# The compression's first weights as units of the weight ring, in a fused two-layer kernel on one core

## What is computed

```python
u = rms_norm(h, norm_mix_pre[l])
(q_n, kc_n, vc_n, ks_n, vs_n, kw_n, vw_n, g_n,
 q_s, k_s, v_s, gate_a, gate_b) = jnp.split(u @ w_in[l], IN_OFFSETS, axis=-1)
kc = compress_kv(kvr(kc_n), cmp_pos_k[l], cmp_w1_k[l], cmp_w2_k[l])
vc = compress_kv(kvr(vc_n), cmp_pos_v[l], cmp_w1_v[l], cmp_w2_v[l])
o_a = nsa_attention(q_n..., kc, vc, ks_n, vs_n, kw_n, vw_n, g_n, bias_nsa)
o_b = swa_sink_attention(q_s, k_s, v_s, attn_sinks, bias_swa)
y = sigmoid(gate_a) * (o_a @ w_up_nsa) + sigmoid(gate_b) * (o_b @ w_up_swa)
h = h + rms_norm(y @ w_out, norm_mix_post)
...
def compress_kv(kv, pos, w1, w2):   # 15 overlapping blocks of 32 tokens, 2 groups
    ...
    return jax.nn.gelu(flat @ w1) @ w2      # flat 30 x 2048, w1 2048 x 256
```

## Time and profile before

| | us |
|---|---|
| Median of 3 runs | 1580.57 (1578.18 to 1581.78) |
| The profiled execution | 1580.16 |
| Its span in the trace | 1578.4 |
| Mean granted TensorE clock | 0.987 of 2.4 GHz |
| PE busy | 1525.8 |
| DVE busy | 1028.0 |
| ACT busy | 835.6 |
| POOL busy | 349.9 |
| Read from HBM | 250.23 MB |

### The profile page before, as it was taken

The page is one execution under the profiler, slowest core; times in us unless marked ns, Lnnn a source line. Parts: engine busy times, 40 slices in busy tenths (PEclk is TensorE's granted clock), DMA queues, the critical chain, the costliest instruction groups (busy, mean ns, idle before and its releaser), DMA issues.

```text
span 1578.4 us, 29131 instructions
## 1 busy us (share of the span) xinstructions
PE 1525.8 (97%) x11414; PEld 1428.1 (90%) x11414; DVE 1028.0 (65%) x1792; ACT 835.6 (53%) x1638; POOL 349.9 (22%) x403
## 2 busy tenths in 40 slices
PE   7799999999989989999999999999999999999998
PEld 6389999999988989999999999999999888888886
DVE  4255567555677864577999967777774555555554
ACT  4166455444456543445444457777775555554544
POOL 1132421000255553411455540011112000000000
PEclk9899999999998999999999999999999999999999
DMA  9732354555443532355445554444445555555553
GB/s 213 229 108 95 135 191 162 183 179 186 147 129 101 164 123 81 101 178 192 147 162 175 172 181 153 138 144 137 145 135 171 189 198 189 197 191 197 190 197 135
DMA packets 76773, 254.23 MB, mean 161 GB/s; under 512 B 11375, under 2 KB 15293, under 8 KB 76509
## 3 DMA queue, kind: packets, MB, share of 16 engines
q1 hardware_dynamic: 76397, 251.71, 48.5%
q0 software_dynamic: 240, 0.66, 0.2%
HBM read 250.23 MB, written 1.84 MB: 160 GB/s over the span
## 4 chain that ended last, share of the span: by engine, by line
PE 79%; DVE 12%; DMA 2%; ACT 2%; POOL 2%; issue 1%; SPq 0%; POOLq 0%; DVEq 0%; ACTq 0%
PE bank L675 78%; DVE wl L1667 4%; DVE big L1667 3%; POOL big L2347 1%; DMA big<-in_w1k 1%; ACT big L1242 1%; DVE big L1670 1%; ACT wh L1242 1%; DVE big L2193 1%; DVE big L2204 1%; DVE big L2200 1%; DVE big L2189 1%; DVE big L2210 1%; DVE big L2197 1%; PE bank L990 1%
## 5 line engine op out<-in xcount | busy, mean ns | idle before, releaser
L1667 DVE TENSOR_TENSOR wl<-raw,wh 128x1024 fp32r<-128x1024 f32 (+4 forms) x459 | 532.1, 1160 | 397.5 <-ACT wh L1242 397.0
L1242 ACT ACTIVATE wh<-raw 128x1024 fp32r<-128x1024 f32 (+1 forms) x459 | 482.2, 1053 | 347.9 <-PE bank L675 330.3
L675 PE MATMUL bank<-gw,wh 128*128 128x256 f32 x3504 | 652.8, 288 | 2.7 <-DVE big L1670 2.7
L675 PEld LDWEIGHTS bank<-gw,wh 128*128 128x128 f32 x3504 | 548.7, 193 | 3.5 <-DVE big L1670 3.1
L675 PE MATMUL bank<-gw,wl 128*128 128x256 f32 x1752 | 498.5, 285 | 6.1 <-POOL wl L2347 5.0
L675 PEld LDWEIGHTS bank<-gw,wl 128*128 128x128 f32 x1752 | 337.7, 193 | 7.8 <-issue 6.3
L675 PE MATMUL bank<-xw,wh 128*128 128x256 f32 x1696 | 322.9, 291 | 9.7 <-ACT wh L1242 7.9
L675 PE MATMUL bank<-wh,xw 128*128 128x512 f32 x1056 | 326.9, 391 | 0.0
L675 PEld LDWEIGHTS bank<-xw,wh 128*128 128x128 f32 x1696 | 268.7, 195 | 17.3 <-ACT wh L1242 8.2
L1242 ACT ACTIVATE big<-bank 128x256 f32<-128x256 f32 (+23 forms) x326 | 118.2, 372 | 259.9 <-PE bank L675 221.7
L2347 POOL TENSOR_TENSOR wl<-raw,wh 128x384 fp32r<-128x384 f32 (+3 forms) x131 | 175.4, 1345 | 333.2 <-ACT wh L1242 333.1
(11 more groups left out here) (136 smaller groups left out, 1096.4 us busy)
## 6 DMA issues: line engine op xcount, KB each, us to landing
raw<-in_wst SPq DMA_DIRECT2D x455, 512.0 KB, 3.5
big<-toeplitz SPq DMA_DIRECT2D x8, 256.0 KB, 14.0
big<-in_w1k SPq DMA_DIRECT2D x4, 512.0 KB, 18.3
big<-in_w1v SPq DMA_DIRECT2D x4, 512.0 KB, 19.1
big<-in_xT SPq DMA_DIRECT2D x4, 256.0 KB, 5.4
raw<-in_wst SPq DMA_DIRECT2D x4, 256.0 KB, 5.1
big<-in_keys SPq DMA_DIRECT2D x1, 1024.0 KB, 5.4
out<-big SPq DMA_DIRECT2D x4, 256.0 KB, 2.4
```

What stands on the lines that cost most here:

```text
L675: return e.matmul(o, a, b, start=first, stop=last, skip_group_check=True)
L1242: return e.activation(o, x, f, **kw)
L1667: return e.tensor_tensor(o, a, b, f)
```

## The change

1. The eight pieces of w1 become units 14, 16, ..., 28 of the ring (`W1_AT`); UNITS goes from 457 to 465. Each shares a slot with an ordinary unit before it (13, 15, 17, 19: queries of the second attention; 21 to 27: four of the `GA` gates). They are split into halves as all units are, and TensorE's new `compress` makes 8 products for each behind the slot's last quarter: the inputs' high and low halves side by side (60 columns) by `WH`, and the high half (30 columns) by `WL`. The inputs' halves are `CXW`, in the free second half of `GW`: two copies on ScalarE and two subtractions on VectorE. `H60` takes the sums; four products with `I2` (two identities above each other) add high and low parts and transpose, in place of four transposes; gelu comes behind them.
2. Order of units: first the selected and window keys (0, 1), then queries (2 to 5), then kc and vc (6, 7). All from the up projection on is 8 units higher and otherwise in the old order.
3. Attention starts at unit 12 instead of 9; its turns run through all slots from there. `finish` is at (turn 5, quarter 2) instead of (turn 6, quarter 3). The compression ends in slots 29 to 35 and is added to `OA` last, and not first. Values use bank 6 alone; the compression has bank 7.
4. SP's order: the copy to `toeplitz` stands ahead of units 4 to 7; rows and units alternate; small constants come behind unit 15; `first_w1` is gone.

The diff, cut to its core:

```diff
-KC, VC, KSL, KWN, QN0, TM, KSW, QS0, GA, GB = 0, 1, 2, 3, 4, 8, 12, 13, 17, 25
-UPA, UPB, WO, MLP = 33, 37, 41, 49
+KSL, KWN, QN0, KC, VC, TM, KSW, GA4, GB = 0, 1, 2, 6, 7, 8, 12, 29, 33
+UPA, UPB, WO, MLP = 41, 45, 49, 57
...
-PAIRS = (KC, WO, MLP, XA, DU, MX, QU)
+W1_AT = {14 + 2 * n: ("kv"[n // 4], n % 4) for n in range(8)}
+QS_AT = [13, 15, 17, 19]
+GA_AT = [21, 23, 25, 27, *range(GA4, GB)]
...
+PAIRS = (KSL, *QS_AT, *GA_AT[:4], WO, MLP, XA, DU, MX, QU)
...
+        CXW = {x: flat(GW[:, 4 + 2 * n:6 + 2 * n, :]).rearrange("p (j c) -> p j c", c=64) for n, x in enumerate("kv")}
...
-        ATT_AT = [9, 10, 11, 12, 13] + list(range(17, 30))
+        ATT_AT = [12, *QS_AT, *GA_AT, *range(GB, GB + 5)]
-        FEATURES_AT = {22: 1, 26: 3, 28: 4, 30: 5}
+        FEATURES_AT = {GB + 2: 1, GB + 3: 3, GB + 4: 4, GB + 5: 5}
...
+                        elif u in W1_AT:
+                            x, j = W1_AT[u]
+                            src = I["w1k"] if x == "k" else I["w1v"]
+                            e.dma_start(r.rearrange("p (a b) -> p a b", b=256), src[:, 4 * j:4 * j + 4, :]).then_inc(
+                                *load[u % RR].sent(u))
...
+                def compress(u):
+                    x, j = W1_AT[u]
+                    col = slice(0, 256) if x == "k" else slice(256, 512)
+                    if j == 0:
+                        e.wait_ge(*cmA.at("x" + x))
+                        e.wait_ge(*cmD.at("l" + x))
...
+                    e.wait_ge(*hi.at(u))
+                    for c in range(4):
+                        w = slice(256 * c, 256 * c + 256)
+                        mm(banks[7][0:60, col], CXW[x][:, 4 * j + c, 0:60], WH[:, u % RW, w], j == 0 and c == 0, False)
+                        if c == 0:
+                            lo_ready(u)
+                        z = mm(banks[7][0:30, col], CXW[x][:, 4 * j + c, 0:30], WL[:, u % RW, w], False, j == 3 and c == 3)
+                    z.then_inc(*unit.sent(u))
+                def products_and_compress(units):
+                    u = units[0]
+                    for q, _ in enumerate(products(u, banks[bank_of(u)][:, 0:T], XH, XL)):
+                        if q == 3:
+                            compress(units[1])
+                        yield
...
                 def compress_side():
                     b = banks[7]
-                    yield from clock.until(7, 2)
...
-                            z = mm(b[0:30, T * i:T * i + T], x[:, j, :], w[:, j, :], j == 0, j == 15)
...
-                    yield from clock.until(12, 1)
+                    yield from clock.until(GA4, 2)
...
-                        z = e.transpose(b[:, 32 * i:32 * i + 30], HTM[:, half(i)], ident[0:30, 0:30])
+                        z = mm(b[:, 32 * i:32 * i + 30], H60[:, half(i)], I2)
...
-                    yield from clock.until(6, 1)
-                    e.wait_ge(*s_l1.at("sel"))
+                    yield from clock.until(11, 1)
+                    e.wait_ge(*s_pos.at(0))
...
+                    for x, src in (("k", CX), ("v", CV)):
+                        e.wait_ge(*cmA.at("x" + x))
+                        tt(CXW[x][:, :, 30:60], src, CXW[x][:, :, 0:30].bitcast(F32), ALU.subtract).then_inc(*cmD.sent("l" + x))
...
-                        yield from clock.until(u, 3)
-                        for s in at_turn(turn - 6):
+                        yield from clock.until(u, 2)
+                        for s in at_turn(turn - 5):
                             finish(s)
```

More of the change, by code:

```diff
@@ L312, in program @@
         unit = steps("unit", range(UP + 125))
-        evD = steps("ev_dve", [u for u in range(DN) if u < TM or KSW <= u < WO or XA <= u < CK or PU <= u < PGB or u >= DU])
+        evD = steps("ev_dve", [u for u in range(DN) if u < TM or (KSW <= u < WO and u not in W1_AT) or XA <= u < CK or PU <= u < PGB or u >= DU])
         evA = steps("ev_act", [u for u in range(UP) if WO <= u < MLP or u in HID.values()
@@ L600, in _ @@
                 weights(2, 4)
-                e.dma_start(POS, I["pos"]).then_inc(*s_l1.sent("pos"))
+                e.wait_ge(*biD.at(0))
+                e.dma_start(toep, VBIAS[:, None, :].broadcast_to([16, 16, 384])).then_inc(*s_toepw.sent(0))
+                weights(4, 8)
+                e.wait_ge(*s_toepw.at(0))
+                for a in range(6):
+                    bias_rows(a)
+                    weights(8 + a, 9 + a)
+                for u, dst in ((KC, KC2), (VC, VC2)):
+                    e.wait_ge(*evD.at(u))
+                    e.dma_start(dst[64:128, 0, 0:256], dst[0:64, 0, 1:257]).then_inc(*s_swap[u].sent(0))
+                    e.dma_start(dst[0:64, 1, 1:257], dst[64:128, 1, 0:256]).then_inc(*s_swap[u].sent(1))
+                e.dma_start(POS, I["pos"]).then_inc(*s_pos.sent(0))
+                bias_rows(6)
+                weights(14, 15)
+                bias_rows(7)
+                weights(15, 16)
                 e.dma_start(W2K, I["w2k"]).then_inc(*s_l1.sent("w2k"))
@@ L938, in compress_side @@
                     z.then_inc(*cmP.sent("kv"))
-                    yield from clock.until(13, 2)
+                    yield from clock.until(GA4 + 2, 2)
                     e.wait_ge(*cmA.at("vcs"))
@@ L1009, in values @@
                         for j in range(nb):
-                            z = columns(banks[6 + run % 2][:, 64 * h:64 * h + 64], PTS[s % 4][:, half(m * nb + j)],
+                            z = columns(banks[6][:, 64 * h:64 * h + 64], PTS[s % 4][:, half(m * nb + j)],
                                         V[:, j, v:v + 64], j == 0, j == nb - 1)
@@ L1192, in topk_side @@
                     b = banks[7]
-                    yield from clock.until(190 + 56, 0)
+                    yield from clock.until(QU + 61, 0)
                     e.wait_ge(*tkD.at((7, "red", 1)))
@@ L1200, in topk_side @@
                     z.then_inc(*tkP.sent("ids"))
-                    yield from clock.until(190 + 56, 3)
+                    yield from clock.until(QU + 61, 3)
                     e.wait_ge(*tkD.at("gate"))
@@ L1456, in features @@
                     e.wait_ge(*tfP.at(run))
-                    act(GH[:, c:c + 4, half(tile)], quad(banks[6 + run % 2]), AF.Copy).then_inc(*tfA.sent(run))
+                    act(GH[:, c:c + 4, half(tile)], quad(banks[7]), AF.Copy).then_inc(*tfA.sent(run))
                 def mlp_stat_side():
@@ L1462, in mlp_stat_side @@
                         square(2, c, H[:, c, :])
-                    yield from clock.until(59, 0)
+                    yield from clock.until(MLP + 10, 0)
                     spread(2)
@@ L2215, in topk_side @@
                     alone = (("ta",), ("tb",), ("tc",), ("td",), ("tf",))
-                    yield from clock.until(190, 0)
+                    yield from clock.until(QU + 5, 0)
                     e.wait_ge(*s_l3.at("iota16"))
@@ L2250, in topk_side @@
                     tt(TS, TS, R8[:, :, :, None].broadcast_to([128, 2, 8, 16]), ALU.subtract).then_inc(*tkD.sent("sub"))
-                    yield from clock.until(190 + 55, 0)
+                    yield from clock.until(QU + 60, 0)
                     reduce_picked(7)
@@ L2401, in mlp_stat_side @@
                 def mlp_stat_side():
-                    yield from clock.until(57, 0)
+                    yield from clock.until(MLP + 8, 0)
                     power(2)
@@ L2532, in topk_side @@
                         t = 26 * h + 23
-                        yield from clock.until(190 + t // 4, t % 4)
+                        yield from clock.until(QU + 5 + t // 4, t % 4)
                         e.wait_ge(*tkD.at((h, "upos")))
```

300 lines of the change are left out of this document (141 added, 159 removed).

## The result

The changed kernel took 1563.98 us (median of 4 executions, 1562.18 to 1567.47) against 1580.01 for the kernel before (1578.18 to 1581.78): ratio 0.9901, interval 0.9880 to 0.9922. That is 16.0 us faster, where the prediction said 20.45, and inside its range of 1554 to 1569. The profiled execution took 1564.18 us (span 1562.4). What was to go went. The question is the 4 us that did not come.

The account below looks back on a forecast made before the run. TensorE, busy 97% of the span, was taken as the bound. -11.25 - 19.9 + 7.7 - 2.0 + 3.0 + 2.0 = -20.45 us, from 1580.16 to 1559.7 us, range 1554 to 1569.

Parts of the forecast that it names:

- The idle stretch (-11.25): TensorE's idle time from 38.85 to 50.10, waiting for compression's first weights (in_w1k), goes: 11.25 us less.
- the old waits (-2.0): TensorE's waits for VectorE ahead of the transposes go, as bias results are ready earlier: 2.0 us less.
- The products (-19.9): The 32 fp32 compression products between 50.10 and 83.50 go, 0.62 us each with slow clock and changeovers: 19.9 us less.
- the new ones (+7.7): 64 narrow fp32r products on TensorE's queue, 8 in each new unit, at 0.12 us each: 7.7 us more.
- The end of the compression (+2.0): Compression's chain in slots 29 to 35 gives some results 0.5 to 0.7 us late: 2.0 us more, between 0 and 5.
- (b): Rival: the paired slots are bound by handovers, 1 us more in each of eight slots, 1567.7 us; chance 0.15.
- (d): Rival: the 64 narrow products cost what the old did, 32.1 us more, 1591.8 us, slower; chance 0.03.
- (e): Rival: a 3 us wait lets TensorE's granted clock fall, 1.4 us more, 1561.1; chance 0.45 together with the forecast.
- (c): Rival: the idle stretch only moves to units 13 to 15, the same bytes being queued, 1568.0 us; chance 0.08.
- The new waits at units 13 and 15 (+3.0): TensorE waits up to 1 us for unit 13's bank and 1.9 us for attention biases: 3.0 us more, between 0 and 6.
- 1.5 us of delay in the queue: Upper correction to the last bias row's arrival, as units 4 and 5 wait for the copy to toeplitz: up to +1.5 us.

Follow-up runs that it names:

- before_10of32: The kernel before with 22 of the 32 fp32 products of compression's first layer left out: 1570.68 us, ratio 0.9938.
- results_first: The changed kernel with ScalarE's copies of compression's inputs moved behind unit 12's token results: 1566.72 us, ratio 0.9924.
- units_first: The changed kernel with the loads of units 4 and 5 issued ahead of SyncE's wait for the bias table: 1566.74 us, ratio 0.9916.
- rows_spread: The changed kernel with each of the eight bias loads writing every eighth partition instead of 16 neighbouring ones: 1557.54 us, ratio 0.9850.
- the aligned run: The changed kernel with the bias rows' 1 KB pieces starting at multiples of 64 bytes, bias values wrong: 1561.04 us in one execution.
- after_rows_16k: The changed kernel with the eight bias loads reading 16 KB pieces from a weight tensor, bias values wrong: 1563.10 us, ratio 0.9887.

## Why the forecast held, and where it was 4 us off

**The idle stretch (-11.25), the old waits (-2.0).** Right: neither shows among the waits.

**The products (-19.9) and the new ones (+7.7).** Right. Eight narrow products take 0.93 us, 7.4 us in all. The token units took 11.35 us without their one short wait (43.17 to 54.78, less 0.26), where 11.5 were reckoned. before_10of32 measured 0.47 us a product, while the account of the whole needs the 19.9, as below. The Trainium skill's four passes for fp32 ("FP8 and Floating Point Precision", TensorE Precision Notes) make an estimate of 0.48 us each and 15.4 for all. The trace agrees with it for the product itself.

**The end of the compression (+2.0).** Mis-sized: it cost nothing. The chain of copies, gelu and softmax never made TensorE wait; between 68 and 169 us there is no wait at all. The estimate had the steps' results too late; which step it mistimed stays open.

**Rivals.** (b), handovers in the paired slots: the scores of successive paired slots start at 69.57, 74.20, 79.26 and 84.32, and no slot up to 169 us has a wait. The working against it had a slip: ScalarE's terms add up to 5.65 us and the reads, up to 6.65 and not 6.4, which still fits. (d): 0.115 us a product, not 0.44. (e), the clock: it came, but after another wait than the one named, and cost 1.5 us. The working there held that short waits don't bring it down; in results_first waits of 1.64, 0.99 and 0.64 us within 5 us did, to 0.69 from 70 to 80 us. (c), the same bytes still stand in the queue: this is the one that the prediction sold too cheap, at 0.08. It came by about half.

**The new waits at units 13 and 15 (+3.0).** This is the step that failed. It was to be 1 us at unit 13 (swaps) and 1.9 at the biases (unit 15). In fact 7.1 us came at units 11 to 13 with the slow clock (0.26 + 0.16 + 1.30 + 3.88 + 1.5), none at the biases (ready at 68.4, wanted at 69.57), because unit 13's delay covered them. Its argument was: before, the queue had delivered all rows and unit 9 at 49.97; now units 10 to 14 come in between, each 1.3 us at 407 GB/s. By it the swaps, behind unit 13, land at 50.1; unit 13 landed at 57.25. A queue of rows and units in turn does not run each at the rate that it had alone. From unit 4's landing (23.40) to unit 13's (57.25) it brought nine units and six rows: 25.5 us at 1.3 and 2.3 us each, and it took 33.9. By landings, the last three pairs of a row and a unit took 4.65, 4.51 and 3.51 us where 3.6 each were reckoned.

**A wait that wasn't in the forecast at all.** Units 4 and 5 now stand behind SyncE's wait for the bias table. The prediction had this only as 1.5 us of delay in the queue. It did not ask who waits for unit 4: its low half stands ahead of the mean on VectorE. Cost with the slow clock behind it: 3.6 us (the token units start at 43.17, where 38.85 + 0.72 = 39.57 was reckoned).

**The account at the milestone.** -20.45 + 3.6 (statistics) + 4.1 (7.1 for 3.0) - 2.0 (the tail) - 0.3 (narrow products) = -15.05, against -14.35 measured; 0.7 us is left, which I can't place beyond changeovers around the new groups of products. The two errors of waits are not independent: units_first took the first away and the second grew by as much. As one cause it is the queue: rows_spread returned 6.7 us with one edit of its targets, and with the queue relieved the early issue of units 4 and 5 returned 4.4 us. That the number came out within 4 us is in part luck: a wait put too low by 4.1 and one left out (3.6) were met by a tail put too high by 2.0.

What stays open: what the starts of the pieces cost, since the aligned run is a single execution and aligned to 64 bytes alone; what still holds the queue once the loads are spread; and whether the old unit order is worth anything, as its milestones are 1.8 and 0.6 us earlier and no median is.

## What to carry to other kernels

A wait that an edit removes is worth its length only if what comes next is not bound by the same queue; make the check with the rate of the mixture that the queue will hold, not with each load's rate alone. Where DMA engines are full at well under the rate of the large loads, look at which partitions a load writes as well as at its piece size; here the first mattered and the second did not. And ask of every load that an edit delays which half-finished work of another engine stands behind it in order.

## What the runs showed of the hardware

In the expectation of after_rows_16k I had taken the slow bias loads (114 GB/s with the engines full) as a matter of their short pieces. Sixteen times longer pieces into the same 16 neighbouring partitions changed the time by 0.9 us, which is within the spread of the executions; the same short pieces into every eighth partition changed it by 6.4. With the early units in both kernels, the spread targets changed the rate from 30 to 50 us from 169 to 235 GB/s at a share of 1.07.

The Trainium skill has a rule for this in "SBUF — State Buffer", Door 1: The DMA port swizzle: the bandwidth of a DMA depends on how many of the 16 ports its partitions reach, and the port follows from bits 4 to 2 and bit 6 of the partition's number. By it 16 neighbouring partitions reach 4 ports and every eighth partition 8. Its 435 GB/s for 16 ports make an estimate of 109 GB/s for 4 of them, beside the 114 of the trace. The trace agrees within 5%. The runs show that the target partitions matter; that ports are the reason is the page's account, and no run here tells ports from another property of neighbouring partitions. The loss in the mixture (169 GB/s) comes from the runs alone.
